# Mean of squares kept in SBUF by ScalarE for the norms of queries and keys

## Chip, cores and metric

The kernel runs on one core of a Trainium2 chip. The metric is the device time of one execution in microseconds, the median of several runs. The same kernel takes 3142.52 to 3145.22 us in three runs.

## The reference

Two blocks are computed one after the other on 512 tokens of width 1024, in float32. The first has two layers of attention and convolution, with 256 tokens of context beside the 512 in layer 0; the second has a recurrent layer, a sparse attention and two feed-forward layers. What matters here lies in the first block: every head's queries and keys are divided by the root of their mean square over the 64 elements of the head, and multiplied by a gain.

```
def rms_norm(x, g):
    y = x * rsqrt(mean(x * x, axis=-1) + EPS)      # EPS = 1e-6, over 64 elements of a head
    return y * g

q = rms_norm(split_heads(nq, 8), na_q_norm[l])      # neighbourhood branch, queries
k = rms_norm(split_heads(nk, 8), na_k_norm[l])      # and keys, and those of the context
q = axial_rope(rms_norm(split_heads(wq, 8), wa_q_norm[l]), ...)   # windowed branch: normed, then rotated
k = axial_rope(rms_norm(split_heads(wk, 2), wa_k_norm[l]), ...)
```

## The kernel before

The program is one long order of steps for each layer L and branch br (br = 0 is the neighbourhood attention, br = 1 the windowed one), made by `Plan.branch` and walked by every engine in its own function (`pe_attn`, `act_attn`, `dve_attn` and one for GpSimd). An engine executes its part of the order strictly in turn and waits on semaphores: `due(...)` gives the waits for the events named, `did(...)` records an event at the end of an instruction.

A projection of 128 output features ("lin", line 1795) takes eight steps, each of three matmuls for every range of tokens (the weights and the activations are split into a high and a low part). ScalarE rounds each weight chunk (line 1106) and VectorE makes its low part (line 1116). The result stands in a pair of PSUM banks. While attention runs, pairs 2 and 3 are lent to the scores, so pairs 0 and 1 serve everything else: `pairs.take` hands out the pair that has been idle longest, `pairs.release` says which events must have happened before TensorE may write it again.

The norm of a tile of queries ("aq") or keys ("ak") is a chain of steps woven in between the matmuls of the next projection. There are 26 of them: 18 of 768 tokens (text and context) and 8 of 512.

- nrm1: VectorE copies the projection out of PSUM into a buffer q (line 2098), ScalarE squares it into a buffer s (line 2020).
- nrm2: TensorE multiplies the squares by a matrix of ones that sums over each head (line 1836), into a pair of banks called p2. ScalarE takes the logarithm of the mean square plus epsilon from PSUM into a buffer y, in two halves (line 2026), then the exponential of minus half of it, in place (line 2030). That is a first value of the inverse root.
- nrm3: VectorE makes one Newton step (`dve_norm`), each of four instructions on two halves: line 2168 writes -0.5/64 y y into s, line 2172 adds epsilon to the sums in PSUM and multiplies by s, line 2176 adds 1.5 and multiplies by y, line 2180 multiplies q by the gain and y.
- In the windowed branch TensorE then multiplies the normed tile by a rotation matrix (line 1841), and VectorE combines the two (lines 2186 to 2190).
- out: ScalarE, VectorE and GpSimd later write high and low parts of the tile to where the scores read them (lines 2048, 2201, 2270).

The pair p2 is released by line 2172 (event "read"). Beside this the queues hold: scores (lines 1899, 1900) with their exponentials on ScalarE (line 1997) and products with the values (line 1919); row maxima (TensorE lines 1866 and 1872, VectorE lines 2212 to 2225), whose negative goes to the queries as a row by ScalarE (line 2056); the end of a head (ScalarE lines 2079 and 2082, VectorE 2233 to 2239); gates (ScalarE line 1981, a table load ahead of them and one behind, line 1983); and on VectorE the taps of the convolution (line 1636).

Of the kernel before, what the change touches and what calls it, by code (L numbers as in the profile page):

```python
# [17 lines left out]
EPS = 1e-6  # L18
# [247 lines left out]
class Plan:  # L266
# [301 lines left out]
    def attn(self, L, br):  # L568
        order = self.orders[L, br] = self.branch(L, br)
        for i in (2, 3):  # L570
            assert i in self.pairs.idle
        lent = self.pairs.lend([2, 3])
        p2, p3 = lent.slots
        B = self.banks[L, br] = Banks([p2[:, 0:512], p2[:, 512:1024], p3[:, 0:512], p3[:, 512:1024]],
                                      [lent.free[0], lent.free[0], lent.free[1], lent.free[1]])
        pt = self.pts[L, br] = Ring([0, 1])
        turn, tmp, pairs = 0, self.tmp, self.pairs
        for u in order:
            kind, nm = u[0], u[1]
            if kind == "lin":  # L580
                if u[2] == 0:
                    woven = nm[0] in ("ak", "aq", "av", "ag") or nm[0] == "mg" and nm[3] < 3 and not br
                    self.linear(nm, [((u[3], u[4], 0, 128 * u[5], POOLED if woven and L and br else 1), list(range(u[5])))])
            elif kind == "nrm1":
                tmp.take((nm, "q"))
                tmp.take((nm, "s"))
                pairs.release(nm, (nm, "q"), (nm, "sq"))
            elif kind == "nrm2":
                pairs.take((nm, "p2"))
                tmp.take((nm, "y"))  # L590
            elif kind == "nrm3":
                pairs.release((nm, "p2"), (nm, "read"))
                tmp.release((nm, "y"), (nm, "y"))
                if not br:
                    tmp.release((nm, "s"), (nm, "y"))
            elif kind == "rot":
                pairs.take((nm, "p3"))
            elif kind == "rot2":
                pairs.release((nm, "p3"), (nm, "b"))
                tmp.release((nm, "s"), (nm, "y2"))  # L600
            elif kind == "out":
                if u[2] == 1:
                    tmp.release((nm, "q"), (nm, "out", 0), (nm, "out", 1))
            elif kind == "vev":
                tmp.take((nm, "v"))
                pairs.release(nm, (nm, "v"))
            elif kind == "vt":
                pairs.take((nm, "t"))
                tmp.release((nm, "v"), (nm, "t"))
            elif kind == "vout":  # L610
                pairs.release((nm, "t"), (nm, "out"))
            elif kind in ("gev", "mgev"):
                tmp.take((nm, "g"))
                pairs.release(nm, (nm, "g"))
            elif kind == "pjev":
                pairs.release(nm, ("yp",) + nm[1:] if br else ("y", L, 0, nm[3]))
                tmp.release((("mg",) + nm[1:], "g"), ("y", L, 2 * br, nm[3]))
            elif kind == "paev":
                pairs.release(nm, ("yc",) + nm[1:])
                tmp.release((("cm",) + nm[1:], "g"), ("y", L, 1, nm[3]))  # L620
            elif kind == "cgev":
                pairs.release(nm, ("cgs", L, nm[3]))
            elif kind == "tick":
                self.tick(*u[1:])
            elif kind == "modend":
                self.mod_end(u[2])
            elif kind == "split" and nm[3] == 0:
                pairs.give_back([2, 3], [listed(B.free[0:2]), listed(B.free[2:4])])
            elif kind == "ln0":
                tmp.take(("csq", L, 0))  # L630
            elif kind == "ln1":
                pairs.take(("mean", L))
                pairs.release(("mean", L), ("cen", L))
                for m in range(1, 4):
                    tmp.take(("csq", L, m))
                    tmp.release(("csq", L, m), ("csa", L, m))
                tmp.release(("csq", L, 0), ("csm", L))
            elif kind == "lnv":
                pairs.take(("var", L))
            elif kind == "ln2":  # L640
                self.rsqrt(("ln", L), ("var", L))
            elif kind == "ln3":
                tmp.release((("ln", L), "y"), ("lny", L, 3))
            elif kind == "max":
                B.take(u, (2 + turn % 2,))
                B.release(u, ("mx",) + u[1:])
                turn += 1
            elif kind == "tr":
                B.take(u, (2 + turn % 2,))
                B.release(u, ("row",) + u[1:])  # L650
                turn += 1
            elif kind == "st":
                p, f, k = u[3:]
                B.take(u, (2 + (turn % 2),))
                turn += 1
                pt.take(u)
                B.release(u, ("ex",) + u[1:])
            elif kind == "pv":
                p, f, k = u[3:]
                if k == 0:  # L660
                    B.take(("o", L, br, p, f), (0, 1) if L == 0 else (f,))
                pt.release(("st",) + u[1:], ("pv",) + u[1:])
            elif kind == "fin":
                B.release(("o",) + u[1:], ("fin",) + u[1:])
            elif kind == "gate":
                if u[4] == 1:
                    tmp.release((("ag", L, br, u[3]), "g"), ("gated", L, br, u[3], 0), ("gated", L, br, u[3], 1))
# [255 lines left out]
def build(nc, t, out):  # L923
# [5 lines left out]
    with ctx:  # L929
# [144 lines left out]
        def buf(name):  # L1074
            return (P.T_ring if name in P.T_ring.slot else P.tmp).of(name)
# [938 lines left out]
        def act_norm(act, L, br, u):  # L2014
            nm = u[1]
            n = tokens(L, nm[0])
            if u[0] == "nrm1":
                for w in due("act", (nm, "q"), was((nm, "s"))):
                    act.wait_ge(*w)
                act.activation(buf((nm, "s"))[:, 0:n], buf((nm, "q"))[:, 0:n], ACT.Square).then_inc(*did("act_nsq", (nm, "sq")))  # L2020
                return
            y, ps = buf((nm, "y")), pairs.of((nm, "p2"))
            for i, h in enumerate((slice(0, n // 2), slice(n // 2, n))):
                for w in due("act", (nm, "sum"), was((nm, "y")), ("eps",)):
                    act.wait_ge(*w)
                act.activation(y[:, h], ps[:, h], ACT.Ln, bias=EPSC[:, 0:1], scale=1.0 / 64).then_inc(*did("act_rs", (nm, "ln", i)))
            for i, h in enumerate((slice(0, n // 2), slice(n // 2, n))):
                for w in due("act", (nm, "ln", i)):
                    act.wait_ge(*w)
                act.activation(y[:, h], y[:, h], ACT.Exp, scale=-0.5).then_inc(*did("act_rs", (nm, "exp", i)))  # L2030
# [129 lines left out]
        def dve_norm(dve, L, br, nm):  # L2160
            n = tokens(L, nm[0])
            q0, y, a, ps = buf((nm, "q")), buf((nm, "y")), buf((nm, "s")), pairs.of((nm, "p2"))
            gain = sm(f"wa_k{L}" if br else f"na_k{L}") if nm[0] == "ak" else QG[L, br][:, 0:1]
            hs = list(enumerate((slice(0, n // 2), slice(n // 2, n))))
            for i, h in hs:
                for w in due("dve", (nm, "exp", i), (nm, "sum")):
                    dve.wait_ge(*w)
                dve.scalar_tensor_tensor(a[:, h], y[:, h], -0.5 / 64, y[:, h], ALU.mult, ALU.mult).then_inc(*did("dve_rs", (nm, "1", i)))
            for i, h in hs:
                for w in due("dve", (nm, "1", i)):  # L2170
                    dve.wait_ge(*w)
                dve.scalar_tensor_tensor(a[:, h], ps[:, h], 64 * EPS, a[:, h], ALU.add, ALU.mult).then_inc(*did("dve_rs", (nm, "2", i), (nm, "read")))
            for i, h in hs:
                for w in due("dve", (nm, "2", i)):
                    dve.wait_ge(*w)
                dve.scalar_tensor_tensor(y[:, h], a[:, h], 1.5, y[:, h], ALU.add, ALU.mult).then_inc(*did("dve_rs", (nm, "3", i)))
            for i, h in hs:
                for w in due("dve", (nm, "3", i), ("qg", L, br), (nm, "sq")):
                    dve.wait_ge(*w)
                dve.scalar_tensor_tensor(q0[:, h], q0[:, h], gain, y[:, h], ALU.mult, ALU.mult).then_inc(*did("dve_rs", (nm, "y")))  # L2180
# [1308 lines left out]
```

## Time and profile before

| | |
|---|---|
| median of three runs | 3142.65 us (3142.52 to 3145.22) |
| the profiled execution | 3145.4 us, of which the span is 3143.6 us |
| mean granted clock of TensorE | 0.994 of full speed |
| TensorE busy | 3029.9 us (96%) |
| VectorE busy | 1858.6 us (59%) |
| ScalarE busy | 1282.9 us (41%) |
| GpSimd busy | 263.7 us (8%) |

In the rows, PE is TensorE's matmul, PEld its load of weights, DVE VectorE, ACT ScalarE and POOL GpSimd. L2172 is line 2172 of the kernel. PS is PSUM, T a buffer in SBUF. Times are in microseconds, means of one instruction in nanoseconds. An arrow points to what ended a wait.

### The profile page before, as it was taken

Reading aid. Unit: us, or ns where it says so; the run is one execution under the profiler, and the core shown is the slowest. Engines: PE = TensorE matmul, PEld = TensorE weight load, DVE = VectorE, ACT = ScalarE, POOL = GpSimd, SP = SyncE. Lnnn points to the kernel's source line nnn. Section 1 sums busy time; section 2 is a strip of 40 time slices with the busy share of each in tenths; the row PEclk is TensorE's granted clock in tenths of the full one; section 3 lists DMA queues with packets and bytes.
Section 4 is the critical chain, followed back from the end, with each engine's and each line's share of the span. In section 5 each row is a group of like instructions: output and inputs, shape, how many; then the busy total and the mean of one; then the engine's idle time right before and its main releaser. Section 6 shows DMA issues by size and latency. Waiting matters only on the chain.

```text
span 3143.6 us, 36963 instructions
## 1 busy us (share of the span) xinstructions
PE 3029.9 (96%) x14782; PEld 2393.2 (76%) x14782; DVE 1858.6 (59%) x2959; ACT 1282.9 (41%) x1989; POOL 263.7 (8%) x206
## 2 busy tenths in 40 slices
PE   8999999999999998999999999999999989999998
PEld 5878877877788676767777777788888866788887
DVE  5877675255435667685443787666435675566632
ACT  3244523135532344534554475322225656422222
POOL 0011100001100001102110031000003210000000
PEclk9999999999999999999999999999999989999999
DMA  5222132320012322222112233232332310233332
GB/s 207 72 69 74 48 101 96 109 86 28 21 34 78 104 81 81 67 81 69 47 54 67 83 99 93 94 94 94 96 96 88 121 38 1 81 94 94 94 94 74
DMA packets 78731, 251.49 MB, mean 80 GB/s; under 512 B 9121, under 2 KB 11169, under 8 KB 78561
## 3 DMA queue, kind: packets, MB, share of 16 engines
q1 hardware_dynamic: 72672, 227.91, 22.9%
q0 software_dynamic: 5024, 18.09, 1.8%
q8 instruction: 117, 1.92, 0.3%
q10 hardware_dynamic: 864, 3.15, 0.3%
q14 instruction: 54, 0.43, 0.0%
HBM read 247.01 MB, written 2.10 MB: 79 GB/s over the span
## 4 chain that ended last, share of the span: by engine, by line
PE 45%; ACT 4%; DVE 3%; issue 1%; DMA 0%; POOL 0%; DVEq 0%; ACTq 0%
PE PS L1157 31%; PE PS L1795 4%; PE PS L2815 3%; PE PS L2910 1%; PE PS L1919 1%; ACT WH L1106 1%; PE PS L2875 0%; PE PS L2891 0%; PE PS L2837 0%; ACT PS L2958 0%; PE PS L2876 0%; PE PS L2892 0%; ACT PTN L2972 0%; ACT L1981 0%; PE PS L2543 0%
## 5 line engine op out<-in xcount | busy, mean ns | idle before, releaser
L1116 DVE TENSOR_TENSOR WL<-RAW,WH 128x1024 fp32r<-128x1024 f32 (+3 forms) x374 | 423.7, 1134 | 527.5 <-ACT WH L1106 526.9
L1106 ACT ACTIVATE WH<-RAW 128x1024 fp32r<-128x1024 f32 (+3 forms) x397 | 384.6, 972 | 435.3 <-PE PS L1157 331.0
L1795 PE MATMUL PS<-Hh,WH 128*128 128x512 f32 x1376 | 525.0, 382 | 14.5 <-DVE WL L1116 7.9
L1795 PE MATMUL PS<-Hl,WH 128*128 128x512 f32 x1376 | 487.4, 354 | 0.0
L1795 PE MATMUL PS<-Hh,WL 128*128 128x512 f32 x1376 | 486.1, 353 | 0.0
L1795 PEld LDWEIGHTS PS<-Hh,WH 128*128 128x128 f32 x1376 | 260.0, 189 | 74.6 <-issue 22.7
L1157 PE MATMUL PS<-XH,WH 128*128 128x512 f32 x768 | 305.1, 397 | 0.0
L1157 PE MATMUL PS<-XH,WL 128*128 128x512 f32 x768 | 303.5, 395 | 0.0
L1157 PE MATMUL PS<-XL,WH 128*128 128x512 f32 x768 | 303.5, 395 | 0.0
L1795 PEld LDWEIGHTS PS<-Hl,WH 128*128 128x128 f32 x1376 | 260.3, 189 | 47.6 <-issue 10.1
L1795 PEld LDWEIGHTS PS<-Hh,WL 128*128 128x128 f32 x1376 | 260.3, 189 | 40.3
L1636 DVE SCALAR_TENSOR_TENSOR C<-AP,SMA,C 128x512 f32<-128x512 f32 x360 | 227.0, 692 | 0.5
L1157 PEld LDWEIGHTS PS<-XL,WH 128*128 128x128 f32 x768 | 144.0, 188 | 36.0 <-issue 1.0
L1157 PEld LDWEIGHTS PS<-XH,WH 128*128 128x128 f32 x768 | 144.0, 188 | 35.9 <-issue 1.0
L1157 PEld LDWEIGHTS PS<-XH,WL 128*128 128x128 f32 x768 | 144.0, 187 | 35.2
L1157 PE MATMUL PS<-FGh,WH 128*128 128x512 f32 x384 | 152.2, 396 | 0.0
L1157 PE MATMUL PS<-FGh,WL 128*128 128x512 f32 x384 | 151.8, 395 | 0.0
L1157 PE MATMUL PS<-FGl,WH 128*128 128x512 f32 x384 | 151.7, 395 | 0.0
L1157 PE MATMUL PS<-Hh,WH 128*128 128x512 f32 (+1 forms) x384 | 138.8, 362 | 2.0 <-DVE Hl L1243 1.9
L1157 PE MATMUL PS<-Hl,WH 128*128 128x512 f32 (+1 forms) x384 | 137.1, 357 | 0.0
L1157 PE MATMUL PS<-Hh,WL 128*128 128x512 f32 (+1 forms) x384 | 137.1, 357 | 0.0
L2472 ACT ACTIVATE U<-U 128x512 f32<-128x512 f32 x48 | 30.4, 633 | 253.1 <-DVE U L2503 253.1
(401 smaller groups left out, 5742.1 us busy)
## 6 DMA issues: line engine op xcount, KB each, us to landing
RAW<-in_w_in SPq DMA_DIRECT2D x124, 512.0 KB, 3.6
RAW<-in_ffn_in SPq DMA_DIRECT2D x96, 512.0 KB, 3.6
RAW<-in_ffn_out SPq DMA_DIRECT2D x48, 512.0 KB, 3.5
RAW<-in_w_ada SPq DMA_DIRECT2D x32, 384.0 KB, 3.7
RAW<-in_nsa_in SPq DMA_DIRECT2D x21, 512.0 KB, 3.3
RAW<-in_lru_in SPq DMA_DIRECT2D x20, 512.0 KB, 3.6
MW<-in_w_ada SPq DMA_DIRECT2D x32, 256.0 KB, 9.7
BS<-in_bs POOLq DMA_DIRECT2D x16, 512.0 KB, 3.9
```

Of the source, the lines that this page charges most:

```text
L1106: act.activation(WH[half[j]][:, 0:n], RAW[j % NRAW][:, 0:n], ACT.Copy).then_inc(*did("act_whi", ("whi", j)))
L1116: dve.tensor_tensor(WL[half[j]][:, 0:n], RAW[j % NRAW][:, 0:n], WH[half[j]][:, 0:n].bitcast(F32), ALU.subtract).then_inc(*did("dve_wlo", ( ...
L1157: mm = pe.matmul(ps[:, c:c + n], wt[:, 128 * i:128 * i + 128], x[:, a:a + n], start=(seen == 0 and q == 0), stop=(seen == total - 1 and q ...
L1636: dve.scalar_tensor_tensor(dst, src, wt, dst, ALU.mult, ALU.add).then_inc(*did("dve_tap", ("tap", L, m, k, a0), ("tap", L, m, k)))
L1795: mm = pe.matmul(ps[:, c:c + w_], wt[:, 128 * k:128 * k + 128], x[:, a:a + w_], start=(k == 0 and q == 0), stop=(k == n - 1 and q == 2))
L1919: mm = pe.matmul(dst, VV[L, br][:, b, 64 * g:64 * g + 128], src, start=first, stop=end)
L2472: act.activation(u, u, ACT.Gelu_apprx_tanh).then_inc(*did("act_ge", (a, "gelu")))
L2815: mm = pe.matmul(ps[:, 0:S], wt[half[j]][:, 128 * k:128 * k + 128], x[:, k, :], start=(k == 0 and q == 0), stop=(k == 7 and q == 2))
L2910: mm = pe.matmul(o[64 * f:64 * f + 64, 0:256].rearrange("p (m q) -> p m q", m=2), VN[b][:, kt, g, :], pt[:, f, :, :], start=(b == 0 and kt ...
```

## The change

ScalarE gets one more instruction in nrm2, between the two logarithms and the two exponentials: over all n tokens it writes 1/64 of the sums plus epsilon from PSUM into the buffer s, whose squares TensorE has read by then. VectorE's first step of the Newton step reads s there, multiplies it by -0.5 and y and writes it back; the second is a product of s and y and reads no PSUM any more. The pair p2 is released in nrm2, once both logarithms and the new instruction are done, no longer in nrm3 after line 2172.

```diff
@@ Plan.attn
             elif kind == "nrm2":
                 pairs.take((nm, "p2"))
                 tmp.take((nm, "y"))
+                pairs.release((nm, "p2"), (nm, "ln", 0), (nm, "ln", 1), (nm, "var"))
             elif kind == "nrm3":
-                pairs.release((nm, "p2"), (nm, "read"))
                 tmp.release((nm, "y"), (nm, "y"))
@@ act_norm
                 act.activation(y[:, h], ps[:, h], ACT.Ln, bias=EPSC[:, 0:1], scale=1.0 / 64).then_inc(*did("act_rs", (nm, "ln", i)))
+            act.activation(buf((nm, "s"))[:, 0:n], ps[:, 0:n], ACT.Identity, bias=EPSC[:, 0:1], scale=1.0 / 64).then_inc(*did("act_rs", (nm, "var")))
             for i, h in enumerate((slice(0, n // 2), slice(n // 2, n))):
@@ dve_norm
             for i, h in hs:
-                for w in due("dve", (nm, "exp", i), (nm, "sum")):
+                for w in due("dve", (nm, "exp", i), (nm, "var")):
                     dve.wait_ge(*w)
-                dve.scalar_tensor_tensor(a[:, h], y[:, h], -0.5 / 64, y[:, h], ALU.mult, ALU.mult).then_inc(*did("dve_rs", (nm, "1", i)))
+                dve.scalar_tensor_tensor(a[:, h], a[:, h], -0.5, y[:, h], ALU.mult, ALU.mult).then_inc(*did("dve_rs", (nm, "1", i)))
             for i, h in hs:
                 for w in due("dve", (nm, "1", i)):
                     dve.wait_ge(*w)
-                dve.scalar_tensor_tensor(a[:, h], ps[:, h], 64 * EPS, a[:, h], ALU.add, ALU.mult).then_inc(*did("dve_rs", (nm, "2", i), (nm, "read")))
+                dve.tensor_tensor(a[:, h], a[:, h], y[:, h], ALU.mult).then_inc(*did("dve_rs", (nm, "2", i)))
```

## Rows read from the trace of the kernel before

**Rows 1.** The chain that ended last, by engine, from the page.
```profile
PE 45%; ACT 4%; DVE 3%; issue 1%; DMA 0%; POOL 0%; DVEq 0%; ACTq 0%
```
**Rows 2.** Waits: engine, line, released by, us in total, times, longest.
```profile
PE PS L1795 <- DVE T L2172: 5.3, 5, 1.3
PE PS L1841 <- DVE T L2180: 4.6, 5, 1.4
...
PEld PS L1795 <- DVE T L2172: 6.9, 5, 1.6
...
DVE T L2168 <- ACT T L2030: 16.2, 9, 4.0
```
**Rows 3.** Timeline, 657 to 663: start, length, engine, line, out and in, idle before.
```profile
657.37 1.05 ACT L2026 ACTIVATE T<-PS,EPSC 128x384 f32<-128x384 f32 x2 [1.75 <-PE PS L1836]
658.31 0.94 ACT L2030 ACTIVATE T<-T 128x384 f32<-128x384 f32 x2
658.87 1.03 DVE L2168 SCALAR_TENSOR_TENSOR T<-T 128x384 f32<-128x384 f32 x2 [1.92 <-ACT T L2030]
...
662.87 0.70 PE L1841 MATMUL PS<-T,CO 128*128 128x512 f32 x1 [1.36 <-DVE T L2180]
```
**Rows 4.** Timeline, a norm of 512 tokens, 1460 to 1462 us.
```profile
1460.55 0.84 ACT L2026 ACTIVATE T<-PS,EPSC 128x256 f32<-128x256 f32 x2 [1.22 <-PE PS L1836]
1461.28 0.72 ACT L2030 ACTIVATE T<-T 128x256 f32<-128x256 f32 x2
1461.73 0.76 DVE L2168 SCALAR_TENSOR_TENSOR T<-T 128x256 f32<-128x256 f32 x2 [3.06 <-ACT T L2030]
```
**Rows 5.** Groups by line and shape, 120 to 1610 us: busy us, mean ns, idle before.
```profile
L2176 DVE SCALAR_TENSOR_TENSOR T<-T 128x384 f32<-128x384 f32 x36 | 18.3, 548 | 0.0
L2172 DVE SCALAR_TENSOR_TENSOR T<-PS,T 128x384 f32<-128x384 f32 x36 | 18.2, 547 | 0.0
...
L1270 ACT ACTIVATE Hh<-T,MOD 128x512 fp32r<-128x512 f32 x8 | 5.7, 723 | 6.9 <-DVE T L1252 6.9
```
**Rows 6.** Timeline, first norm of layer 1's windowed branch.
```profile
1449.68 1.46 DVE L2168 SCALAR_TENSOR_TENSOR T<-T 128x384 f32<-128x384 f32 x2 [3.96 <-ACT T L2030]
```
**Rows 7.** Timeline, ScalarE and TensorE, 254 to 259 us.
```profile
254.47 1.28 ACT L1981 ACT_TABLE_LOAD   x1 [0.52 <-PE PS L1795]
...
255.89 0.50 PE L1795 MATMUL PS<-Hh,WH 128*128 128x512 f32 x1 [1.28 <-DVE T L2172]
...
257.89 0.37 ACT L2056 ACTIVATE QB<-PS 1x256 fp32r<-1x256 f32 x1
...
258.31 0.19 PEld L1899 LDWEIGHTS PS<-QA,KA 128*128 128x128 f32 x1 [0.25 <-ACT QB L2056]
```
**Rows 8.** Timeline, ScalarE and VectorE, 1110 to 1117 us.
```profile
1110.73 0.93 ACT L2030 ACTIVATE T<-T 128x384 f32<-128x384 f32 x2
1111.53 1.02 DVE L2168 SCALAR_TENSOR_TENSOR T<-T 128x384 f32<-128x384 f32 x2
...
1116.71 0.68 DVE L2098 COPY T<-PS 128x512 f32<-128x512 f32 x1
```
**Rows 9.** Timeline, layer 1's neighbourhood branch, 1200 to 1206 us.
```profile
1200.68 1.03 DVE L2168 SCALAR_TENSOR_TENSOR T<-T 128x384 f32<-128x384 f32 x2 [1.44 <-ACT T L2030]
...
1205.15 0.14 DVE L2212 DVE_READ_ACCUMULATOR2_ANT STAT<- 128x1 f32 x1
...
1205.42 0.19 PEld L1866 LDWEIGHTS PS<-KA,QA 128*128 128x128 f32 x1 [0.24 <-DVE STAT L2212]
```
**Rows 10.** Timeline, the first norm of all.
```profile
130.68 0.94 ACT L2030 ACTIVATE T<-T 128x384 f32<-128x384 f32 x2
131.60 1.02 DVE L2168 SCALAR_TENSOR_TENSOR T<-T 128x384 f32<-128x384 f32 x2
```
**Rows 11.** Busy by stretches of 4 us; the granted clock is the third last column.
```profile
1476.00:1480.00 4.00, 2.19 (x11) 1.96 (x11) 3.04 (x5) 0.00 (x0) 0.00 (x0) 0.84 0.24 66
1480.00:1484.00 4.00, 4.00 (x19) 3.27 (x18) 2.16 (x4) 0.89 (x2) 0.00 (x0) 0.73 0.00 0
```

## The prediction

> **What bounds the kernel now.** I read the chain that ended last first: TensorE leads it and ScalarE and VectorE together hold 7% [rows 1]. An edit on those two engines is therefore worth only what it does to a wait of TensorE. So I read who TensorE waited for, and took two rows. It waited 5.3 us, five times, for VectorE's line 2172, the reading of the sums out of PSUM, because the next projection needed that pair of banks. It waited 4.6 us, five times, for line 2180, the end of the norm, before it could rotate the normed tile [rows 2]. The change pulls on these two in opposite senses: line 2172 no longer holds the pair, and everything from the exponential to line 2180 moves behind one more ScalarE instruction. The rest is reading the timeline around each of the 26 norms (18 of 768 tokens, 8 of 512), all of them between 128 and 1605 us; the second block and the convolution hold none of it.
>
> **The new ScalarE instruction.** 26 are added, one over all tokens of each norm, between the two logarithms and the two exponentials. What counts is by how much it puts off the first exponential. Two logarithms of 384 columns, with the same source and the same bias column, move the next instruction by 0.94 us, 0.47 each [rows 3]; two of 256 by 0.73, 0.365 each [rows 4]. The line through both gives 0.79 us for 768 columns and 0.58 for 512. Lower end 0.63 (the columns' part of that line alone, 0.82 ns each), upper end 0.94 (two halves of 384); I take 0.79, since it is one instruction with one fixed part. 26 of them are 19 us of busy time, of which only what reaches TensorE counts. Identity with a bias column already runs in the stretch of line 1270, 723 ns for 512 columns, with no table load of that line beside it [rows 5], so I add no reload.
>
> **VectorE.** Four instructions a half stay four. The second took 547 ns with its sums from PSUM, the third 548 ns with both operands in SBUF [rows 5]; a product of two tensors in their place I price the same, so 0, and the rows leave some 10 ns an instruction either way, 0.2 us in the sum. The Trainium skill ("VectorE: DVE Perf Modes", section on the TRN2 errata) gives VectorE a fixed part of 120 cycles from PSUM and of 58 from SBUF; by that each half would save 65 ns and the sum would be about 1 us less; the rows show no such difference. Upward there is more room: line 2168, with both operands in SBUF, once took 1.46 us for its two halves instead of 1.03 [rows 3, 6], with GpSimd at a weight split beside it; the new second step may meet that too, 0.4 us at a place or two.
>
> **What the earlier release is worth.** The pair comes free after the added instruction, some 2 to 8 us sooner, and the 5.3 us of waits on line 2172 go. What is late next? At four of the five places (255.89 us is the first; 317.06, 1217.28 and 1269.15 repeat it) ScalarE has begun, before TensorE stalls, on a run without any idle: table load at 254.47, gate, table load, and at 257.89 the row of query maxima (line 2056). TensorE's scores wait for that row, and start at 258.31, 0.25 us after their weights could have been loaded [rows 7]. The run starts when an earlier projection ends, so TensorE's 1.28 us of lead is spent waiting at 258.31 instead. Worth 0. At the fifth place, the shortest, at 1113.5 us, VectorE works without idle from line 1636 through the norm to the copy of the next query tile at 1116.71, whose square TensorE needs next [rows 8]. Worth 0 as well.
>
> **What the later exponential costs.** VectorE sat idle for line 2030 nine times, 16.2 us together [rows 2]; at those nine the whole delay lands on VectorE's chain.
> - Four of them are norms of the windowed branch of layer 0 (658.87, 671.17, 767.89, 825.21): chain of line 2168 to line 2180, then the rotation's matmul, which waits (1.36 us at 662.87) [rows 3]. The delay goes through whole: 4 x 0.79 = 3.16.
> - Two in layer 1 (1200.68 and 1252.57): behind the norm VectorE takes the row maxima, and the bank they free is loaded for 0.04 us later than it could have been (a load behind a small matmul shows 0.24 us anyway) [rows 9]. 2 x 0.75 = 1.50.
> - 1449.68: 0.79 less 0.44, since line 2168 would start after GpSimd's instruction had ended and lose its stretched half [rows 6]: 0.35.
> - 1461.73: 0.58, with a slack of 0.03 ahead of the rotation [rows 4]: 0.55.
> - The ninth, 1487.66, is followed by slack: 0.
> Of the other 17, VectorE was late anyway at thirteen; what hides the instruction there is the convolution's taps and the row maxima in VectorE's queue, and without that cover each would cost its 0.79 or 0.58. At four the cover is too short. At 131.60 the first exponential ended at about 131.20, and 131.99 is 0.39 late [rows 10]. At 1111.53 it ended at 1111.25, so 0.51 [rows 8]. At two more, in the same way, the queue behind the exponentials holds a softmax exponential (line 1997) whose product on TensorE has less in hand than the delay: 0.30 at 183.0 and 0.20 at 1155.8 us. Together 1.40.
> Sum: 3.16 + 1.50 + 0.35 + 0.55 + 1.40 = 6.96, against a gain of 0: **+7.0 us**. The profiled execution has a span of 3143.6 us and took 3145.4 us; the median of the runs is 3142.65. I put the sum on the median: **3149.6 us**, 0.22% more.
>
> **A rule against the change.** The sums are read by one VectorE instruction a half. The Trainium skill ("VectorE: DVE Perf Modes", rules for kernel authors) says to copy a matmul's output to SBUF if many operations will read it, and else to accept the slower source. Here one reads it, so by that rule the copy buys no VectorE time, which is what the rows above say too; only the bank's release could pay.
>
> **Rivals.**
> - *The release pays.* If what waits next at the five places is not the dense run that I read, the 5.3 us stay won and the sum is 6.96 - 5.3 = +1.7 us, 3144.3. For it: these are the waits that the change names. Against: the load at 258.31 waits for line 2056 by its own row [rows 7]. Chance 0.20.
> - *Faster.* The release pays in full, weight loads and all (the loads' waits for line 2172 sum to 6.9 us [rows 2]), and the delays on the rotation path are swallowed by later waits of TensorE. That is -6.9 us, 3135.8. The deciding point is the rotation at 662.87: if its wait does not grow from 1.36, this case holds. Against it: ahead of that wait VectorE was idle for the exponential, so nothing covers it. Chance 0.06.
> - *The clock falls.* The wait at 662.87 grows to 2.15 us and that of 675.17 alike. After a wait of 3.01 us at 1477.81 the granted clock was 0.84 in one stretch of 4 us and 0.73 in the next, that is partly 1.2 instead of 2.4 GHz [rows 11]; the work lost is 4 x (0.16 + 0.27) = 1.7 us. At two or three places, +3.4 to +5.1 on top: 3153 to 3154.7. Chance 0.14.
> - *It does not do what it says*: ScalarE reaches the added instruction so late that the pair is no freer. At every one of the 26 it stands right behind the logarithms, so this can't be; and an Identity that reloads tables would add 2.57 us a norm, 67 us, against line 1270's row. Chance 0.02, left out of the range (a table load takes 1.28 us [rows 7]).
>
> **How the numbers follow.** My sum has 0.58. Its own spread: the instruction at 0.63 to 0.94 us makes it 5.6 to 8.3; VectorE from SBUF adds up to 0.8 or takes off 0.2; a few places misread, 2 us either way. So 3146 to 3153 for the likeliest case. With the release's case and the clock's most of it the range is 3143.5 to 3154.5. About 0.2%, 6.3 us, is what a measurement of this kernel can tell from no change, and my sum lies just beyond it: of my 0.58 some 0.36 falls beyond and 0.22 within; the clock's 0.14 and the 0.02 fall beyond, the release's 0.20 within, the faster case's 0.06 beyond on its side. That makes faster 0.06, same 0.42, slower 0.52.
>
> **What would show it.** Right: no wait of TensorE for line 2172's successor; scores at the four places still waiting for line 2056, now by about 1.5 us; the waits for line 2180 up from 4.6 us to about 8; VectorE's idle for the exponential up from 16.2 to about 23; ScalarE busy up by some 20 us; VectorE's busy time the same. Wrong: TensorE's waits for line 2056 or for softmax exponentials unchanged while those on the pair are gone (then the release paid), or a granted clock below 1 around 660 to 680 us.

## The result, and the profile after

The changed kernel took 3157.66 us (median of 6 runs, 3152.6 to 3159.9) beside 3144.22 us for the kernel before on the same chip (6 runs, 3142.5 to 3149.5): ratio 1.0039, 95% interval 1.0026 to 1.0052. It is slower, by 13.4 us where 7.0 were forecast, and lies above the range. (The forecast stood on a median of 3142.65 us from three executions; 13.4 us on top of that is 3156.1, above the range as well.) The profiled executions differ by 11.3 us in span (3154.9 against 3143.6). Lines below 2026 stand one further down: 2172 is now 2173, 2180 is 2181, 2056 is 2057.

First the totals of the page. ScalarE has 19.1 us more, VectorE and TensorE hardly any:

```profile
span 3154.9 us, 36970 instructions
...
PE 3032.8 (96%) x14782; PEld 2393.2 (76%) x14782; DVE 1860.5 (59%) x2959; ACT 1302.0 (41%) x2015; POOL 270.0 (9%) x206
```

The groups by line and shape (busy us, mean ns of one, idle before) price the added and the replaced instruction. The Identity takes 905 ns for 768 columns. The product of two SBUF tensors takes 549 ns, and the reading from PSUM took 547 [rows 5]:

```profile
L2027 ACT ACTIVATE T<-PS,EPSC 128x768 f32<-128x768 f32 x18 | 16.3, 905 | 0.0
...
L2173 DVE TENSOR_TENSOR T<-T 128x384 f32<-128x384 f32 x36 | 18.3, 549 | 0.0
```

The waits (us in total, times, longest) show both halves of the change. The row for line 2172 of [rows 2] has no successor. Its 5.3 us stand nearly whole in the row of line 2057, which was 5.9 us in six waits before. The waits for line 2181 went from 4.6 to 9.1 us, and VectorE waits 26.3 us for the exponential where it waited 16.2:

```profile
PE PS L1899 <- ACT QB L2057: 11.9, 10, 1.8
...
PE PS L1841 <- DVE T L2181: 9.1, 6, 2.3
...
PE PS L1836 <- ACT T L2020: 3.1, 2, 2.3
```

```profile
DVE T L2169 <- ACT T L2031: 26.3, 13, 4.8
```

The timeline around the first rotation answers [rows 3]. Before, the exponentials started 0.94 us behind the logarithms and the rotation waited 1.36 us. Now it is 1.73 us (661.24 less 659.51), and the wait is 2.26:

```profile
659.51 1.05 ACT L2026 ACTIVATE T<-PS,EPSC 128x384 f32<-128x384 f32 x2 [1.75 <-PE PS L1836]
660.46 0.91 ACT L2027 ACTIVATE T<-PS,EPSC 128x768 f32<-128x768 f32 x1
661.24 0.94 ACT L2031 ACTIVATE T<-T 128x384 f32<-128x384 f32 x2
661.81 1.03 DVE L2169 SCALAR_TENSOR_TENSOR T<-T 128x384 f32<-128x384 f32 x2 [2.72 <-ACT T L2031]
...
665.91 1.10 PE L1841 MATMUL PS<-T,CO 128*128 128x512 f32 x2 [2.26 <-DVE T L2181]
```

At 255.89 us, where TensorE had waited 1.28 us for the pair [rows 7], it goes on without a stop, and then meets the row of query maxima at the place where it stood before. The weights that waited 0.25 us now wait 1.80:

```profile
259.39 0.37 ACT L2057 ACTIVATE QB<-PS 1x256 fp32r<-1x256 f32 x1
259.81 0.19 PEld L1899 LDWEIGHTS PS<-QA,KA 128*128 128x128 f32 x1 [1.80 <-ACT QB L2057]
```

**Where the time went.** I matched each matmul of line 1795 with the same one of the kernel before and took the difference of their starts. Where this drift steps up, time is lost. A fall of the clock is a stretch in which TensorE's granted clock is 1.2 instead of 2.4 GHz. The table has the steps, in us, for this kernel and for some experiments told below (times of the places are those of the kernel before; an x marks a step that a fall of the clock is part of):

| place | forecast | changed | e10, the same again | e1, cost only | e5, neighbourhood | e3, windowed | e9, two Identities |
|---|---|---|---|---|---|---|---|
| 139.7 | 0.39 | 0.44 | 0.44 | 0.42 | 0.43 | 0.01 | 1.39 |
| 184.1 | 0.30 | 0.46 | 0.46 | 0.46 | 0.46 | 0.00 | 1.39 |
| 640 to 900, four rotations | 3.16 | 3.46 | 5.07 x | 3.09 | -0.03 | 3.42 | 12.21 x |
| 1110 to 1119 | 0.51 | 0.57 | 0.80 x | 0.56 | 0.57 | 0.00 | 1.78 x |
| 1150 to 1162 | 0.20 | 0.33 | 0.34 | 0.35 | 0.34 | 0.01 | 1.06 |
| 1202 to 1209 and 1253 to 1261 | 1.50 | 1.41 | 1.42 | 1.40 | 1.41 | 0.03 | 3.29 |
| 1453 to 1455 | 0.35 | 0.44 | 0.43 | 0.36 | -0.44 | 0.43 | 1.37 |
| 1464 to 1466 | 0.55 | 0.65 | 0.65 | 0.57 | 0.00 | 0.65 | 1.37 |
| sum | 6.96 | 7.76 | 9.61 x | 7.21 | | | |
| all of 1097 to 1284 | 2.21 | 4.14 x | 4.24 x | 2.57 | 4.13 x | 0.04 | 10.23 x |
| 1284 to 1300 | 0 | 1.54 x | 1.53 x | 0.00 | 1.54 x | -0.01 | 1.53 x |

So the forecast's places hold, with 7.8 us for 7.0. The rest is not at a norm. Between 1119 and 1130 us, and again between 1284 and 1300, about 1.5 us is lost while TensorE computes. Busy time and granted clock (the third column from the end) in stretches of the changed kernel show it:

```profile
1120.00:1124.00 4.00, 1.88 (x12) 1.45 (x10) 3.49 (x7) 0.48 (x1) 0.00 (x0) 1.00 0.00 0
1124.00:1128.00 4.00, 3.79 (x11) 2.84 (x12) 2.87 (x5) 3.13 (x7) 0.00 (x0) 0.65 0.17 18
...
1294.00:1298.00 4.00, 1.97 (x11) 1.36 (x9) 2.81 (x6) 2.38 (x4) 0.00 (x0) 1.00 0.12 34
1298.00:1302.00 4.00, 3.95 (x13) 3.26 (x14) 3.82 (x8) 0.00 (x0) 2.10 (x3) 0.66 0.35 95
```

From 1124 us TensorE is busy, yet the granted clock averages 0.65: it ran at 1.2 instead of 2.4 GHz for 3.4 us. Just before, it was busy for 1.88 of 4 us, since it waited 2.32 us for a square:

```profile
1124.20 1.13 PE L1836 MATMUL PS<-T,CO 128*128 128x512 f32 x2 [2.32 <-ACT T L2020]
```

In the kernel before there were two waits, with 3.4 us of matmuls between them (1113.53 to 1116.98 us), as its waits between 1108 and 1128 us show:

```profile
PE PS L1836 <- ACT T L2020: 1.1, 1, 1.1
PE PS L1795 <- DVE T L2172: 0.3, 1, 0.3
```

With the cost alone (e12, below) the one on the pair is 0.9 us. The release took it away, and its time is spent at the other.

The fall at 1299 is another case, for no wait became longer there. The kernel before has the same wait for the row maxima. Here are its row and that of the changed kernel:

```profile
1288.38 0.44 PE L1866 MATMUL PS<-KA,QA 128*128 128x128 f32 x2 [2.07 <-DVE STAT L2212]
1298.05 0.44 PE L1866 MATMUL PS<-KA,QA 128*128 128x128 f32 x2 [2.07 <-DVE STAT L2213]
```

The busy times around it are also the same as those from 1294 to 1302 us above, but the clock stays at 1.00 in the kernel before:

```profile
1284.33:1288.33 4.00, 1.98 (x11) 1.37 (x9) 2.81 (x6) 2.38 (x4) 0.00 (x0) 1.00 0.12 40
1288.33:1292.33 4.00, 3.95 (x21) 3.18 (x22) 3.81 (x8) 0.00 (x0) 2.10 (x2) 1.00 0.31 94
```

This wait stands at 2.1 us in every profile without fillers at it. The fall follows it in the six that release the pair early in the neighbourhood branches and have no fillers (the changed kernel, e2, e5, e8, e9, e10), and in none of the five that release it as before (the kernel before, e1, e3, e7, e12). What links the two is open.

Falls of the clock, found in the same way: in the kernel before at 642.5, 1478.7, 1656.2, 2519.8 and 2564.2 us; in the changed one at 643.9, 1125.2, 1299.3, 1490.4 (twice as long), 1671.3, 1920.5, 2534.9 and 2575.9. The fall near 1480 (1490 in the changed kernel) also stands behind a wait of the same 3.0 us in both kernels.

One profile of each kernel is not enough to count its falls: e1 and e12 are the same kernel, and the fall near 1480 lasts 6.8 us in one and 3.4 in the other. At 1700 us the drift is 14.0 us. It ends at 11.3, since the fall of before at 2519.8 lasted 13.7 us and that of the changed kernel 3.4; the second profile of the changed kernel (e10) has the 13.7 too, and gives nothing back.

The mean granted clock of every execution helps here. It is 0.9922 in the eleven of the changed kernel (this measurement and e10), 0.9932 in the seventeen of the cost alone (e1 and e12), and 0.9936 in 68 of the kernel before. One more execution of the kernel before, with 3693.62 us at a clock of 0.751, is left out here and in the ratios. Among executions of one kernel (173 in all) the time grows by about 2.4 us for each 0.001 of clock. From these numbers I estimate that the clock takes 3.5 us of the changed kernel's cost and 1.1 us of the cost alone's, and that some 10 and 8 us are left for the rest.

### The profile page after: what moved, and what is told of

It reads as the page before. It is cut to its first block, busy times and chain, and to the rows that moved or that the text cites. A ratio compares the mean times of both kernels' runs of the same rounds, so it can differ in the third digit from the quotient of the medians.

```text
span 3154.9 us, 36970 instructions
## 1 busy us (share of the span) xinstructions
PE 3032.8 (96%) x14782; PEld 2393.2 (76%) x14782; DVE 1860.5 (59%) x2959; ACT 1302.0 (41%) x2015; POOL 270.0 (9%) x206
## 4 chain that ended last, share of the span: by engine, by line
PE 44%; ACT 4%; DVE 3%; issue 1%; DMA 0%; POOL 0%; DVEq 0%; ACTq 0%
PE PS L1157 31%; PE PS L1795 4%; PE PS L2816 2%; PE PS L2911 1%; PE PS L1919 1%; ACT WH L1106 1%; PE PS L2892 0%; PE PS L2838 0%; PE PS L2876 0%; ACT PS L2959 0%; PE PS L2877 0%; PE PS L2893 0%; ACT PTN L2973 0%; ACT L1981 0%; PE PS L2544 0%
```

## Experiments

Theory after the result: the norms pay the delay of the exponential, some 8 us; the release gives nothing; and the rest, 3 to 5 us, is TensorE's clock, which falls at places where the changed waits have become long (of the three places told above, only the one at 1125 has a longer wait). All medians stand beside those of the kernel before on the same chip.

**e1: the cost alone, and e12: the same again.** The Identity behind the logarithms; the release and VectorE's reads as before.

```diff
+            act.activation(buf((nm, "s"))[:, 0:n], ps[:, 0:n], ACT.Identity, bias=EPSC[:, 0:1], scale=1.0 / 64)...
```

> The added ScalarE instruction alone: it runs behind the logarithms in all 26 norms, but VectorE's step still reads PSUM as before and overwrites what it wrote, and the pair of banks is still released by line 2172's successor. Theory (the release is worth nothing, the later exponential is the whole cost): +8 to +11 us, ratio 1.0025 to 1.0035, about the change itself or a little less, since the two waits near 1113 and 1118 us are not joined into one and the clock need not fall there; TensorE's waits for the pair grow from 5.3 to some 9 us. Rival (the release paid 5.3 us of the change's time): the cost alone is 5 us more than the change, +17 us, ratio 1.0055.

Measured 3154.27 against 3145.66 us, ratio 1.0025 (1.0016 to 1.0035). The steps are in the table: 7.21 us in sum, 2.57 between 1097 and 1284, nothing to 1300, and no fall at 1125 or 1299. The time is where theory put it.

> e1 again (the added ScalarE instruction, and the release and the reads of before), beside the changed kernel on one chip: is the changed kernel slower than the one that only pays the cost? Theory (the release brings nothing at the four places, and in layer 1's neighbourhood branch it joins two waits into one of 2.3 us behind which the clock falls): e12 has no fall at 1125 and 1299 us, and its median is 2 to 4 us below e10's. Rival (the release is worth nothing either way): medians within 1 us.

3155.05 against 3144.75, ratio 1.0033 (1.0022 to 1.0045), and 4.4 us below e10 on the same chip, where 2 to 4 were expected; the intervals of the two ratios overlap (e10 has 1.0031 to 1.0058). Waits of e12:

```profile
PE PS L1841 <- DVE T L2181: 8.6, 6, 2.2
PE PS L1795 <- DVE T L2173: 8.4, 5, 2.1
```

Without the release the waits on the pair would have grown from 5.3 to 8.4 us. With it they are gone, and the kernel is no faster for it: 8.4 us of waits removed, 0 gained, and two falls of the clock (1.5 us each) that the profiles without it lack.

**e2: the release alone.** The release behind the logarithms, no Identity, and VectorE's second step reads SBUF; the norms' value of mean square plus epsilon is left out, so that step works on other data.

```diff
+                pairs.release((nm, "p2"), (nm, "ln", 0), (nm, "ln", 1))
+                dve.scalar_tensor_tensor(a[:, h], a[:, h], -0.5, y[:, h], ALU.mult, ALU.mult)...
-                dve.scalar_tensor_tensor(a[:, h], ps[:, h], 64 * EPS, a[:, h], ALU.add, ALU.mult)...
+                dve.tensor_tensor(a[:, h], a[:, h], y[:, h], ALU.mult)...
```

> The release alone: the pair comes free behind the two logarithms and VectorE reads no PSUM, but nothing writes the mean of squares, so VectorE's step works on the squares that stand in its buffer and the norms come out wrong: that part of the computation is left out. Theory: TensorE's 5.3 us of waits for the pair are gone and its waits for line 2056 are up from 5.9 to about 11; time within 2 us of before, ratio 0.9995 to 1.0007. Rival (the release pays): -5.3 us, ratio 0.9983.

3144.87 us, ratio 0.9997 (0.9988 to 1.0007). The waits for the pair are gone here too, and stand where theory put them:

```profile
PE PS L1899 <- ACT QB L2056: 11.9, 10, 1.8
```

This is the changed kernel's row to the tenth. A release without any cost does not bring 5.3 us: the interval reaches from 3.8 us less to 2.2 us more. Its profile also has the fall at 1295 us with its 1.53 us, but not the one at 1125, where its joined wait was 1.8 us. So the fall at 1299 needs neither the Identity nor the fall at 1125. This profile drifts by 7.0 us at 1700 us, with a median like that of before, for it happens to have more falls than the one profile of the kernel before.

**e3: the windowed branches alone, and e5: the neighbourhood branches alone.**

```diff
+            if br:   # e3; in e5: if not br
```

> The whole change in the windowed branches alone, whose norms are followed by the rotation; the neighbourhood branches are as before. Theory: waits of TensorE for the end of the norm go from 4.6 to 9.1 us, those for the pair and for line 2056 stay at 5.3 and 5.9; +4.5 us, and up to 1.4 more if the fall of the clock near 1480 us gets longer: ratio 1.0014 to 1.0019. Rival (the cost is spread by the added 20 us of ScalarE work): in proportion to the norms, 10 of 26, +4.7 us as well, but with the steps between the norms and not at the rotations.

> The change in the neighbourhood branches alone; the windowed branches keep the norm of before. It is the complement of e3. Theory (each norm costs its own delay, and the two clock falls at 1125 and 1299 us belong to the neighbourhood norms of layer 1): places at 139.7, 184.1, 288.1, 1118.7, 1158, 1206 and 1258 us sum to 3.9 us, the two falls add 2.7: drift 6.5 to 7.5 at 1300 us, none at the rotations, ratio 1.0015 to 1.0025. Rival (the falls come from the whole kernel having shifted by then): no falls at 1125 and 1299, drift about 4 to 4.5 at 1300 us, ratio 1.0010 to 1.0014.

e3: 3152.74 against 3145.66, ratio 1.0020 (1.0010 to 1.0029), a little above the expectation; e5: 3148.32 against 3144.75, 1.0014 (1.0005 to 1.0023), a little below and at the upper end of the rival's. The two together give 1.0034, near the whole. Their columns divide the table cleanly. What decides e5 for the theory is its profile: both falls, at 1125 and at 1299, are there without a changed windowed norm, so they come with the changed neighbourhood branches. (Its drift at 1300 us is 8.3 us, not 6.5 to 7.5, with a fall at 228 that the profile before lacks.) But these falls do not make e5 slower as a whole: it lacks those near 1480 and 1656, and the mean granted clock of its eleven executions, 0.9938, is that of the kernel before on the same chip.

**e10: the changed kernel again, e11: one set of fillers, e4: three, e6: three in the kernel before.** A filler is a matmul into unused PSUM that keeps TensorE busy ahead of a wait; the kernel before has some too. The numbers in the edit are issued twice at a place: the six of e11 are twelve matmuls in its trace, 2.75 us from 1120.72 us on.

```diff
+    ('nrm2', ('aq', 1, 0, 0)): 6,          # e11, e4, e6: ahead of the wait at 1122 us
+    ('max', 1, 0, 3, 0, 3): 6,             # e4, e6: near 1297 us
-    ('max', 1, 1, 0, 0, 2): 3,
+    ('max', 1, 1, 0, 0, 2): 8,             # e4, e6: near 1488 us
```

> The changed kernel, unchanged, with more rounds and a second profile, beside e11 and e12 on one chip. Theory (its falls of the clock belong to its stalls and come again): falls at about 1125, 1299 and 1490 us again, drift 14 at 1700 us, ratio 1.0033 to 1.0042. Rival (they were the luck of one profile): other places, drift under 10 at 1300 us, ratio as e12's.

> The changed kernel with six filler matmuls ahead of the first sum of squares of the query norm of layer 1's neighbourhood branch, where its wait is 2.3 us, and nowhere else. Theory (the fall at 1125 us follows that long wait, the one at 1299 follows the wait for the maxima there): the fall at 1125 is gone and saves 1.4 us, those at 1299 and 1490 stay: drift 1.2 to 1.6 below e10's, ratio 0.0004 to 0.0005 below e10's. Rival (the falls hang together, one brings the next): all three go, 4 us or more less than e10.

> The change with six filler matmuls put ahead of each of the waits that end at 1124 and 1297 us in the changed kernel, and five more ahead of the one near 1490 us. Theory (some 4 us of the change's time are three stretches at the lower clock that before did not have, each behind a wait that TensorE spent idle): the granted clock stays 1.00 at 1124 to 1132 and at 1298 to 1306 us, worth 1.4 us each, and the fall near 1490 goes back to what before had: +8 to +9.5 us, ratio 1.0025 to 1.0030. Rival (the clock falls wherever it likes, whatever the waits are): the falls stay or come elsewhere, and the ratio is that of the change, 1.0039, or more by the fillers.

> The kernel before with the filler matmuls of e4 at the same three places and without the change: it shows what the fillers are worth by themselves. Theory (the fillers only keep the granted clock up where the changed kernel stalls longer): before has no fall at 1125 and 1299 us and one after 1478, so the fillers bring at most the 1.7 us of that one and cost at most 1 us of their own time: ratio to before 0.9994 to 1.0003, and e4 against it costs the same 7 to 9 us as the change without its falls. Rival (the fillers speed up any kernel of this kind, and e4's gain over the changed kernel says nothing of the change): ratio 0.9985 or less, that is 4 us or more faster.

| kernel | ratio (95%) | drift 1097 to 1284 | 1284 to 1300 | falls at 1125, 1299 |
|---|---|---|---|---|
| e10 | 1.0044 (1.0031 to 1.0058) | 4.24 | 1.53 | both |
| e11 | 1.0034 (1.0021 to 1.0047) | 2.61 | -0.01 | none |
| e4 | 1.0020 (1.0011 to 1.0030) | 2.60 | 0.24 | none |
| e6 | 1.0001 (0.9993 to 1.0010) | 2.81, of which 1.55 is a fall at 1074 | 0.24 | none |

e10 repeats the falls. In e11 two of the three falls are gone, and with them 3.1 us, not 1.4; its stretch from 1097 to 1300 is that of e1. That is more than the theory said and less than the rival, for the fall near 1490 stayed (6.8 us). The same stretches of e11:

```profile
1120.00:1124.00 4.00, 4.00 (x21) 3.21 (x19) 2.48 (x5) 1.48 (x2) 0.00 (x0) 1.00 0.00 0
1124.00:1128.00 4.00, 4.00 (x22) 3.32 (x21) 3.87 (x8) 2.12 (x6) 0.00 (x0) 1.00 0.37 104
...
1294.00:1298.00 4.00, 2.50 (x12) 2.14 (x13) 3.88 (x10) 0.00 (x0) 0.78 (x2) 1.00 0.25 66
```

Why the fall at 1299 is gone too stays open: its wait was not touched, and this is one profile. e6 shows that the fillers bring nothing in sum to the kernel before: they cost 1.2 us at 1116 and 0.2 near 1290 and spare it the fall near 1480. So what e4 gains over the changed kernel belongs to the changed kernel's falls. e4 has no fall near 1490 either, and its drift goes down by 1.6 us there. With the fillers the change costs 7.0 us, less than the 8 to 9.5 expected and just what was forecast for a kernel without new falls. The ratios of e4 and e10 hardly overlap (1.0011 to 1.0030 and 1.0031 to 1.0058). They come from two chips, but each has the kernel before beside it.

Two of these profiles (e4 and e10), and e12, have what the prediction's third rival asked for: a fall behind the lengthened waits for the rotation. Of e10:

```profile
676.00:680.00 4.00, 1.74 (x8) 1.32 (x8) 3.28 (x7) 0.00 (x0) 0.00 (x0) 0.90 0.09 36
680.00:684.00 4.00, 4.00 (x15) 2.65 (x13) 1.98 (x3) 0.80 (x2) 0.34 (x1) 0.67 0.00 0
```

It costs 1.6 us (5.07 against 3.46 in the table). It comes in three of the seven profiles in which the four rotations wait one Identity longer, in none of the four with the waits of before.

**e7 and e8: the sums of squares of layer 0's windowed branch one step of the projection earlier,** in the kernel before and in the changed one.

```diff
-            c = {8: [("nrm1", nm)], 11: [("nrm2", nm)], ...
+            c = {8: [("nrm1", nm)], 10 if br and L == 0 else 11: [("nrm2", nm)], ...
```

> The kernel before; in the windowed branch of layer 0 TensorE computes the sum of squares one step of the projection earlier (0.87 us). Theory (the rotation waits for the chain sum, logarithm, exponential, four VectorE steps): the waits for line 2180 near 662.9, 675.2, 771.9 and 829.2 us (1.36, 1.36, 0.4, 0.5) shrink by 0.87 each or to nothing, 2.6 us less in all, unless the sum then waits for its square; ratio to before 0.9990 to 0.9995. Rival (what is late behind the rotation is something else, such as the next projection's weights, and takes the time back): waits for line 2180 shrink but the time is that of before, 0.9997 to 1.0005.

> The changed kernel with the sum of squares of layer 0's windowed branch one step earlier. Theory (the change costs 0.84 us at each of these four norms because the exponential comes 0.79 later): the earlier sum takes back 0.87 at each, 3.3 to 3.5 us in all, the waits for line 2181 fall from 9.1 to about 5.6 us, and the ratio to before goes from 1.0039 to 1.0028. Rival (the cost there is contention of the extra ScalarE instruction and not its place in the chain): the drift at the four places stays at 3.3 us and the ratio at 1.0039.

e7: 3145.57 against 3145.56, ratio 1.0001 (0.9992 to 1.0010). Its waits:

```profile
PE PS L1836 <- ACT T L2020: 2.1, 3, 1.1
PE PS L1841 <- DVE T L2180: 1.2, 3, 0.6
```

The waits for line 2180 fell from 4.6 to 1.2 us, but the sum now waits for its square, and another row, line 1848 for line 2020, went from 6.6 to 7.8. The four rotations gained 1.25 us instead of 2.6, and the median shows none of it. e8: 3156.52, ratio 1.0035 (1.0022 to 1.0047); its drift over the four rotations is 1.11 us where the changed kernel has 3.46. So 2.35 of the cost there is place in the chain and can be moved, less than the 3.3 to 3.5 expected, since here too the sum waits for its square (0.68 us at 669.43); the ratio's interval is too wide to show it. No version tried beats the kernel before.

**e9: a double dose.** A second Identity behind the first, which waits for it.

```diff
+            act.activation(buf((nm, "s"))[:, 0:n], ps[:, 0:n], ACT.Identity, ...).then_inc(*did("act_rs", (nm, "dum")))
```

> The changed kernel with the added ScalarE instruction issued twice, the second waiting for the first: a dose. Theory (what the change costs is the delay of the exponentials): where the first delay went through whole, at the four rotations and at 1203 and 1255 us, another 0.9 to 1.0 us each (6 us), some 0.9 each at the places with short cover (4 us), and up to 3 us at places where the cover now runs out: drift against before at 1700 us from 14 to 25 or more, ratio to before 1.0065 to 1.0085. Rival (the cost comes from anything that the instruction does once, such as the missing second half's overlap): under 4 us more, ratio up to 1.0052.

3175.16 us, ratio 1.0097 (1.0084 to 1.0111), more than the theory said. Away from the rotations the second one costs 0.93 to 0.95 us at each norm of 768 tokens with no fall beside it (139.7: 1.39 - 0.44; 184.1; 1206; 1257; 1454) and 0.72 at that of 512 (1465), with 0.73 at 1156 and 1.21 at 1118, where a fall begins. So there it is delay and goes through whole. The rotations are where the expectation was too small:

```profile
PE PS L1841 <- DVE T L2184: 14.5, 6, 3.2
```

Waits of up to 3.2 us, and falls at 672.3, 685.9 (twice as long) and 788.3 us: 12.2 us in place of some 7.

## Why the prediction was wrong, point by point

**What bounds the kernel, and which waits the change touches: right.** All that was lost is lost in TensorE's waits and clock.

**The new instruction: right.** It moves the exponential by 0.79 us (1.73 less 0.94), as the line through [rows 3] and [rows 4] said; its busy time of 905 ns is more, since the next instruction starts before it ends. The Trainium skill ("ScalarE: Activation LUTs", section What ACT_TABLE_LOAD costs) gives an activation with a bias column about 280 ns and 0.833 ns a column, and says that such instructions overlap by about 93 ns. By that it would be an estimated 920 ns, an estimated 827 of them seen by the next one; the trace has 905 and 0.79 us, a little below.

**VectorE: right.** 549 ns for 547. The Trainium skill ("VectorE: DVE Perf Modes", section on the TRN2 errata) gives VectorE a smaller fixed part from SBUF, by an estimated 65 ns; this trace does not agree.

**The release, 0: right about its gain, at all five places.** e2 shows it without the cost (its drift falls by 1.53 us at 255.9 and is up by 1.56 again at 258.9), and e1 against e11 between 1097 and 1300 us with it (2.57 and 2.60 us). What I did not ask is what a wait does that two waits did not. At 1113.5 us I wrote that TensorE's lead is worth 0, and stopped. The two stops became one of 2.3 us.

**The later exponential, 6.96: close at each place, 7.76 in sum.** The rotations cost 3.46 for 3.16. The four places with short cover cost 1.80 for 1.40, each a little more than I had read. One item was right by luck: at 1449.68 us [rows 6] I took the stretched 1.46 us of line 2168 as part of the kernel. In e5 and e7, whose norms there are those of before, it takes 1.03 us and the kernel stands 0.44 us lower. The row of e7:

```profile
1453.02 1.03 DVE L2168 SCALAR_TENSOR_TENSOR T<-T 128x384 f32<-128x384 f32 x2 [3.97 <-ACT T L2030]
```

In e7 GpSimd's instruction ended at 1452.20, before line 2168 began. Against such a run the change costs 0.87 there. A single stretched instruction of one profile is no term of a sum before it is seen twice. In the same way the step of 0.58 us at 288 us in the changed kernel is not its own: e2, e6 and e7, which lack the Identity, have it, and e1, e3, e5 and e10 don't.

**The step that failed: the clock.** I gave it 0.14, at 662.87 and 675.17 us, and nowhere else, and looked for it only where my own sum made a wait longer. It came elsewhere. At 1125 us (1.5 us, in all four profiles with the whole neighbourhood change, one Identity and no fillers: the changed kernel, e5, e8, e10) it fell behind a wait that the release had joined from two. At 1299 us (1.5 us, in the same four) and near 1490 us, where the fall behind the wait for the maxima [rows 11] took 6.8 us instead of 3.4 (1.6 us), it fell behind waits that the change had left as they were, 2.07 and 3.0 us. The second length comes and goes: six of the eight profiles with changed windowed norms and no fillers there have it. At 662 to 680 it comes in some executions only. My price, 1.7 us a fall, was near the 1.5 to 1.6 measured; the count in the profile was three, not none.

7.8 at the norms, 3.1 and 1.6 for these falls, 0.6 at 288 us and 0.5 from the start make 13.6 of the 14.0 us at 1700. That the median's 13.4 is near this sum is luck in part: the last two items, 1.1 us, are not the change's own, and the one profile of the kernel before has few falls. The profile's 11.3 is smaller by what the long fall of before at 2519.8 gave back. Over all executions the clock takes an estimated 3.5 us, and with fillers at the three places (e4) the change costs 7.0 us.

For the fall at 1125 the numbers were there to see it: the waits of 0.3 and 1.1 us in the kernel before, joined by the release that I had just argued for, and the 0.79 us of delay make 2.2 us; measured were 2.3, more than the 2.15 us at 662.87 that I did price a fall for. For the other two there was no longer wait to see, since theirs did not change.

## What to carry to other kernels

When a change removes a stall and the next stall takes its time, write down the length of the one that is left: TensorE computed between the two before, and here its clock fell behind the joined one. Price the clock at every place where a wait grows or two waits join, and not only at the longest; and leave room in the range for falls behind waits that the change does not touch. Do not count falls from one profile of each kernel: compare the mean granted clock over all executions. A copy out of PSUM that frees a bank early costs its length to what is queued behind it, and is worth only the part of the stall behind which nothing else is late.

## What the runs showed of the hardware

At 1125 and 1299 us the granted clock fell from 2.4 to 1.2 GHz for 3.4 us after stretches of 4 us in which TensorE was busy for 1.9 to 2.0 us, with a longest wait of 2.1 or 2.3 us; [rows 11] had a wait of 3.0 us. Neither figure decides it. The kernel before has the same wait of 2.07 us and the same 1.98 of 4 us at 1288 us, and no fall. After the same wait of 2.3 us at 664 us the changed kernel's first profile has no fall, and e10's has one behind the next rotation. e1 and e12, the same kernel, have falls of 6.8 and 3.4 us behind the same wait of 3.0 us. Where twelve filler matmuls filled one wait (e11), the fall there was gone, and so was another 174 us later; the second is not explained.

Over the executions of one kernel the time grows by about 2.4 us for each 0.001 that the mean granted clock is lower.

A release without cost (e2) left the time as it was (0.9988 to 1.0007), though it removed five waits of up to 1.3 us.
